# Fetching the selected value rows of the last 128 tokens instead of computing them densely

## What is computed

```python
v1, i1 = lax.top_k(s1, 16)          # per token and head, 8 heads
v2, i2 = lax.top_k(s2, 16)
...
eidx = take_along_axis(i1 * 128 + i2, pos)      # 16 experts of 16384 per head
g = jax.nn.softmax(top_s, axis=-1)
...
u = eu[it]                                      # 128 rows of 1024 per token
a = gelu(einsum('ckd,cd->ck', u, ht)) * gt
out = einsum('ck,ckd->cd', a, ev[it])           # 128 rows of 1024 per token
```

## Time and profile before

| | |
|---|---|
| median of 3 runs | 1881.18 us (1879.13 to 1882.46) |
| the profiled execution | 1878.64 us, its span 1876.9 us |
| mean granted clock of TensorE | 0.989 of full speed |
| instructions | 25250 |
| moved by DMA | 324.25 MB, mean 173 GB/s |

### The profile page before, as it was taken

One profiled execution on the slowest core, in us unless ns is written; L12 is line 12 of the kernel. 1 busy time (PEld: TensorE's weight loads), 2 busy tenths in 40 slices (PEclk: granted clock), 3 DMA queues, 4 the chain that ended last, 5 costly groups with the idle time before them and its releaser, 6 DMA issues.

```text
span 1876.9 us, 25250 instructions
## 1 busy us (share of the span) xinstructions
PE 1846.2 (98%) x8376; PEld 1511.2 (81%) x8376; DVE 1180.1 (63%) x1792; ACT 712.7 (38%) x938; POOL 762.4 (41%) x327
## 2 busy tenths in 40 slices
PE   5999998999999999999999999999999999999999
PEld 3876677888888888888888888888888888888887
DVE  7575557889990598989898983334434444334444
ACT  3544333334433444444454543232222322322321
POOL 4432223335444343333334344444444444444442
PEclk8999998999999999999999999999999999999999
DMA  7324343224444446464655467455665555665553
GB/s 272 135 80 142 133 151 135 91 79 144 148 145 150 135 163 224 168 218 162 223 179 207 173 212 256 164 196 185 201 204 182 195 190 184 198 203 191 195 180 116
DMA packets 159724, 324.25 MB, mean 173 GB/s; under 512 B 10816, under 2 KB 76480, under 8 KB 157504
## 3 DMA queue, kind: packets, MB, share of 16 engines
q1 hardware_dynamic: 159680, 323.70, 50.9%
HBM read 254.46 MB, written 69.21 MB: 172 GB/s over the span
## 4 chain that ended last, share of the span: by engine, by line
PE 95%; DVE 3%; DMA 1%; issue 0%; ACT 0%; DVEq 0%; SPq 0%; ACTq 0%; PEldq 0%
PE ps L1201 16%; PE ps L1202 16%; PE ps L1203 16%; PE ps L1478 12%; PE ps L1479 12%; PE ps L1477 12%; PE ps L1441 3%; DVE adasum L823 1%; PE ps L1330 1%; PE ps L1348 1%; PE ps L1412 1%; DMA ada<-w_ada 1%; PE ps L1270 1%; PE ps L1339 0%; DMA xt<-x_t 0%
## 5 line engine op out<-in xcount | busy, mean ns | idle before, releaser
L509 POOL TENSOR_TENSOR wlo<-raw,whi 128x1024 fp32r<-128x1024 f32 x304 | 750.5, 2470 | 1089.7 <-ACT whi L540 1089.7
L1201 PE MATMUL ps<-ahi,whi 128*128 128x512 f32 x1296 | 510.0, 394 | 0.2 <-DVE zbuf L917 0.2
L1202 PE MATMUL ps<-alo,whi 128*128 128x512 f32 x1296 | 507.6, 392 | 0.0
L1203 PE MATMUL ps<-ahi,wlo 128*128 128x512 f32 x1296 | 506.9, 391 | 0.0
L540 ACT ACTIVATE whi<-raw 128x1024 fp32r<-128x1024 f32 x304 | 323.6, 1065 | 464.3 <-PE ps L1479 432.1
L1152 DVE TENSOR_TENSOR prod<-gin,gates 128x512 f32<-128x512 f32 x128 | 179.0, 1399 | 403.3 <-DMA gin<-gelu_spill 400.2
L1478 PE MATMUL ps<-plo,whi 128*128 128x512 f32 x1024 | 398.8, 389 | 0.0
L1479 PE MATMUL ps<-phi,wlo 128*128 128x512 f32 x1024 | 398.8, 389 | 0.0
L1477 PE MATMUL ps<-phi,whi 128*128 128x512 f32 x1024 | 398.8, 389 | 0.0
L1203 PEld LDWEIGHTS ps<-ahi,wlo 128*128 128x128 f32 x1296 | 244.6, 189 | 51.6
L1201 PEld LDWEIGHTS ps<-ahi,whi 128*128 128x128 f32 x1296 | 244.9, 189 | 49.3 <-issue 0.7
(11 more groups left out here) (201 smaller groups left out, 1348.1 us busy)
## 6 DMA issues: line engine op xcount, KB each, us to landing
raw<-w_stream SPq DMA_DIRECT2D x304, 512.0 KB, 3.6
gelu_spill<-gout SPq DMA_DIRECT2D x128, 256.0 KB, 3.3
gate_spill<-gblock SPq DMA_DIRECT2D x16, 2048.0 KB, 7.3
gates<-gate_spill SPq DMA_DIRECT2D x32, 1024.0 KB, 7.0
gin<-gelu_spill SPq DMA_DIRECT2D x128, 256.0 KB, 3.8
ada<-w_ada SPq DMA_DIRECT2D x48, 512.0 KB, 5.3
xt<-x_t SPq DMA_DIRECT2D x1, 2048.0 KB, 7.9
out_t<-xt SPq DMA_DIRECT2D x8, 256.0 KB, 2.0
```

The costliest lines, as they stand in the source:

```text
L509: g.tensor_tensor(wlo[:, s, :], raw[:, s, :], whi[:, s, :].bitcast(F32), ALU.subtract)\
L1201: mm(out, shi, mhi, start=n == 0, stop=False)
L1202: mm(out, shi, mlo, start=False, stop=False)
L1203: last = mm(out, slo, mhi, start=False, stop=n == len(pairs) - 1)
```

## The change

The tokens are divided. Tokens 0 to 383 (`DENSE`) keep the dense last stage, with matmuls, products and loads over 384 columns in place of 512, and the scatter has 48 groups in place of 64, among 72 U chunks (`U_B` = 44, `U_C` = 116; 8 groups per 12). The U stage itself still covers all 512 tokens.

For tokens 384 to 511, which sit one to a partition, DVE works out two offsets for each of their 128 selected experts: the row of `w_front` that holds the expert_v row, and the place of its gelu value in `gelu_spill`. In the V stage POOL, after each subtraction, issues two indirect DMAs: `fetch_row(n)` brings expert n's row for each of the 128 tokens (128 x 4 KB) into one of `ROWS` = 8 buffers, `fetch_coef(n)` brings the 128 gelu values (4 bytes each). Row fetches begin at key 0, behind waits for the offsets, the scatter and the gate stores; coefficient fetches begin at key 4, once all gelu values are stored, two per key until they have caught up. DVE, five keys behind (`BEHIND`), multiplies gelu value and gate, and adds the scaled row to `acc`; in the last five keys it adds two. When all 128 are added (`row_added`), PE transposes `acc` into columns 384 to 511 of each bank, behind its last matmuls.

The gate spill is laid out by groups of four keys, so that a load reads 6 KB per partition in one piece, and a store writes pieces of 512 B.

```diff
--- before.py
+++ after.py
@@ -64,9 +64,15 @@
-U_A2, U_B, U_C = 36, 40, 120
-BODY_CHUNKS = 20
-BODY_GROUPS = 16
+DENSE = 3 * P
+FETCHED = TT - 1
+ROWS = 8
+BEHIND = 5
+U_A2, U_B, U_C = 36, 44, 116
+BODY_CHUNKS = 12
+BODY_GROUPS = 8
+GROUPS = DENSE // TOK_GROUP
 TAKE_GROUPS = 8
@@ -77,7 +83,7 @@
     gelu_dram = nc.dram_tensor("gelu_spill", (NK, P, T), F32).ap()
-    gate_dram = nc.dram_tensor("gate_spill", (T // TOK_BLOCK, P, NK * TOK_BLOCK), F32).ap()
+    gate_dram = nc.dram_tensor("gate_spill", (NK // GROUP, P, DENSE // TOK_BLOCK, GROUP * TOK_BLOCK), F32).ap()
@@ -197,11 +203,21 @@
-        gates = at("gates", 78, [P, 2, T // TOK_BLOCK, GROUP * TOK_BLOCK], F32)
-        gin = at("gin", 94, [P, RING, T], F32)
-        prod = at("prod", 8, [P, 2, T], F32)
-        phi = at("phi", 22, [P, RING, T], F32R)
-        plo = at("plo", 30, [P, RING, T], F32R)
+        gates = at("gates", 78, [P, 2, DENSE // TOK_BLOCK, GROUP * TOK_BLOCK], F32)
+        gin = at("gin", 94, [P, RING, DENSE], F32)
+        prod = at("prod", 8, [P, 2, DENSE], F32)
+        phi = at("phi", 22, [P, RING, DENSE], F32R)
+        plo = at("plo", 30, [P, RING, DENSE], F32R)
+        rows = at("rows", 38, [P, ROWS, D], F32)
+        acc = at("acc", 70, [P, D], F32)
+        expert = at("expert", 102, [P, 3, P], F32)
+        row_at = at("row_at", 103.5, [P, P], U32)
+        coef_at = at("coef_at", 104, [P, P], U32)
+        coef = at("coef", 104.5, [P, P], F32)
+        gate_of = at("gate_of", 105, [P, P], F32)
+        scaled = at("scaled", 105.5, [P, ROWS], F32)
+        token = sb("token", [P, 1], F32)
...
@@ -342,12 +363,12 @@
             t0 = s % GROUP * TOK_GROUP + half * 4
-            return gblock[:, s // GROUP % 2, :].rearrange("p (i t) -> p t i", t=TOK_BLOCK)[:, t0:t0 + 4, :]
+            return gblock[:, s // GROUP % 2, :].rearrange("p (i t) -> p i t", t=TOK_BLOCK)[:, :, t0:t0 + 4]
             both = ps[:, 2 * half:2 * half + 2, :].rearrange("p b (t n) -> p (b t) n", n=2 * NK)
-            return both[:, :, part * NK:(part + 1) * NK]
+            return both[:, :, part * NK:(part + 1) * NK].rearrange("p t n -> p n t")
@@ -418,7 +439,9 @@
                 sp.wait_ge(scat_added, 8 * b + 10)
-                sp.dma_start(gate_dram[b], gblock[:, buf, :]).then_inc(gate_stored[buf], 16)
+                sp.dma_start(gate_dram.rearrange("g p b n -> b p g n")[b],
+                             gblock[:, buf, :].rearrange("p (g n) -> p g n", n=GROUP * TOK_BLOCK))\
+                  .then_inc(gate_stored[buf], 16)
@@ -431,16 +454,14 @@
             def gin_load(e, s):
-                sp.dma_start(gin[:, s, :], gelu_dram[e]).then_inc(gin_in[s], 16)
+                sp.dma_start(gin[:, s, :], gelu_dram[e][:, 0:DENSE]).then_inc(gin_in[s], 16)
             def gate_load(g, buf):
-                sp.dma_start(gates[:, buf, :, :],
-                             gate_dram.rearrange("b p n -> p b n")[:, :, bass.ts(g, GROUP * TOK_BLOCK)])\
-                  .then_inc(gate_in[buf], 16)
+                sp.dma_start(gates[:, buf, :, :], gate_dram[g]).then_inc(gate_in[buf], 16)
             for b in range(2):
-                sp.wait_ge(gate_stored[b], 16 * (T // TOK_BLOCK // 2 + 1))
+                sp.wait_ge(gate_stored[b], 16 * (DENSE // TOK_BLOCK // 2 + 1))
             for b in range(2):
@@ -515,6 +536,10 @@
                             pattern=[[-1, HEADS], [0, P]], channel_multiplier=1).then_inc(consts, 1)
+            pool.wait_ge(consts, 15)
+            g.iota(token[:, :], [[0, 1]], base=FETCHED * P, channel_multiplier=1,
+                   allow_small_or_imprecise_dtypes=True).then_inc(token_ready, 1)
+            pool.wait_ge(token_ready, 1)
@@ -523,9 +548,39 @@
                          .then_inc(alo_first_ready, 1)
-            with pool.Fori(1, (C_E + NK) // RING) as i:
+            with pool.Fori(1, C_E // RING) as i:
                 for s in range(RING):
                     lo_part(i * RING + s, s)
+            def fetch_row(n):
+                if n >= ROWS:
+                    pool.wait_ge(row_added, n - ROWS + 1)
+                g.indirect_dma_start(rows[:, n % ROWS, :], None, w_front.rearrange("c p n -> (c p) n"),
+                                     bass.IndirectOffsetOnAxis(row_at[:, n:n + 1], 0)).then_inc(row_in[n % ROWS], 16)
+            def fetch_coef(n):
+                g.indirect_dma_start(coef[:, n:n + 1], None,
+                                     gelu_dram.rearrange("e p (t o) -> (e p t) o", o=1),
+                                     bass.IndirectOffsetOnAxis(coef_at[:, n:n + 1], 0)).then_inc(coef_in[n % ROWS], 16)
+            for e in range(NK):
+                lo_part(C_E + e, e % RING)
+                if e == 0:
+                    pool.wait_ge(places_ready, 1)
+                    pool.wait_ge(scat_done, 4 + 2 * GROUPS)
+                    for b in range(2):
+                        pool.wait_ge(gate_stored[b], 16 * (DENSE // TOK_BLOCK // 2 + 1))
+                fetch_row(e)
+                if e == RING:
+                    for s in range(RING):
+                        pool.wait_ge(gelu_stored[s], 16 * (NK // RING + 1))
+                if RING <= e < ROWS:
+                    for n in (2 * (e - RING), 2 * (e - RING) + 1):
+                        fetch_coef(n)
+                elif e >= ROWS:
+                    fetch_coef(e)
@@ -721,7 +776,7 @@
                     act.wait_ge(slots_done, 1)
-                    a.activation(gate_hi[:, :], ps[:, 2, :], ACT.Copy).then_inc(gate_hi_ready, 1)
+                    a.activation(gate_hi[:, 0:DENSE], ps[:, 2, 0:DENSE], ACT.Copy).then_inc(gate_hi_ready, 1)
@@ -1086,11 +1141,21 @@
                             ALU.mult).then_inc(gates_ready, 1)
+            fetched = [picked[:, k, FETCHED * P:T] for k in range(3)]
+            dve.wait_ge(token_ready, 1)
+            v.scalar_tensor_tensor(expert[:, 0, :], fetched[0], float(NK), fetched[1], ALU.mult, ALU.add)
+            dve.drain()
+            v.tensor_scalar(expert[:, 1, :], expert[:, 0, :], float(C_E * P), None, ALU.add)
+            v.tensor_scalar(expert[:, 2, :], expert[:, 0, :], float(T), token[:, 0:1], ALU.mult, ALU.add)
+            v.tensor_copy(gate_of[:, :], fetched[2])
+            dve.drain()
+            v.tensor_copy(row_at[:, :], expert[:, 1, :])
+            v.tensor_copy(coef_at[:, :], expert[:, 2, :]).then_inc(places_ready, 1)
             dve.wait_ge(slots_done, 1)
             for k in range(2):
-                v.tensor_copy(slots[:, k, :], ps[:, k, :]).then_inc(slots_taken, 1)
+                v.tensor_copy(slots[:, k, 0:DENSE], ps[:, k, 0:DENSE]).then_inc(slots_taken, 1)
             dve.wait_ge(gate_hi_ready, 1)
-            v.tensor_tensor(gate_lo[:, :], ps[:, 2, :], gate_hi[:, :].bitcast(F32), ALU.subtract)\
+            v.tensor_tensor(gate_lo[:, 0:DENSE], ps[:, 2, 0:DENSE], gate_hi[:, 0:DENSE].bitcast(F32), ALU.subtract)\
              .then_inc(slots_taken, 1)
@@ -1137,7 +1202,7 @@
             make_onehots(0, 0)
-            takes = T // TOK_GROUP // TAKE_GROUPS
+            takes = GROUPS // TAKE_GROUPS
             with dve.Fori(0, takes - 1) as i:
@@ -1162,22 +1227,49 @@
-            dve.wait_ge(scat_done, 4 + 2 * (T // TOK_GROUP))
+            def add_row(n, q, s):
+                dve.wait_ge(row_in[s], 16 * (q + 1))
+                dve.wait_ge(coef_in[s], 16 * (q + 1))
+                column = slice(n, n + 1) if isinstance(n, int) else bass.ds(n, 1)
+                v.tensor_tensor(scaled[:, s:s + 1], coef[:, column], gate_of[:, column], ALU.mult)
+                dve.drain()
+                if isinstance(n, int) and n == 0:
+                    v.tensor_scalar(acc[:, :], rows[:, s, :], scaled[:, s:s + 1], None, ALU.mult).then_inc(row_added, 1)
+                else:
+                    v.scalar_tensor_tensor(acc[:, :], rows[:, s, :], scaled[:, s:s + 1], acc[:, :],
+                                           ALU.mult, ALU.add).then_inc(row_added, 1)
+            def last_rows(s):
+                done = NK - 8 - BEHIND + s + max(0, s - (8 - BEHIND))
+                return range(done, done + (1 if s < 8 - BEHIND else 2))
+            dve.wait_ge(scat_done, 4 + 2 * GROUPS)
             for e in range(2):
                 make_prod(None, 0, e)
-            with dve.Fori(0, NK // 8 - 1) as i:
+            for e in range(8):
+                prod_lo(e, e)
+                gates_landed((e + 2) // 8, (e + 2) % 8)
+                make_prod(e + 2, (e + 2) // RING, (e + 2) % 8)
+                if e >= BEHIND:
+                    add_row(e - BEHIND, 0, e - BEHIND)
+            with dve.Fori(1, NK // 8 - 1) as i:
                 for s in range(8):
                     make_prod(i * 8 + n, i * 2 + n // RING, n % 8)
+                    add_row(i * 8 + (s - BEHIND), i + (s - BEHIND) // 8, (s - BEHIND) % 8)
             for s in range(8):
                     make_prod(e + 2, (e + 2) // RING, (e + 2) % 8)
+                for n in last_rows(s):
```

(20 more changed lines are left out.)

## The result

The changed kernel takes 1895.5 us (median of 4 runs, 1890.89 to 1896.27) against 1880.16 for the kernel before beside it: a ratio of 1.0077, 95% interval 1.0064 to 1.0089. It is slower by 15 us where 65 fewer were forecast. The profiled execution took 1896.27, its span 1894.5. One execution of all those in this document (the fourth of the tenth experiment: 2788.6 us, mean granted clock 0.65, where the others have 0.99) was in a slower state and is left out.

The account below looks back on a forecast made before the run. PE bounds the kernel before; afterwards POOL's and DVE's shared access, 5.1 us per key. Scatter -15, last stage -56, start and end +6: -65 from 1878.6 gives 1814, or 1816 us at the median; range 1778 to 1915.

Parts of the forecast that it names:

- B: POOL's queue, last stage: the fetches' issue cost decides; past 1.35 us each POOL sets the pace; chance 0.26.
- D: Last stage: a fetch also excludes DVE's two-input work; 7.4 us per key, 2110 us; chance 0.05.
- PE's part: Last-stage matmuls over 384 columns: 0.173 us each, 4.15 us per key in place of 5.44.
- The scatter: Scatter on PE's path: 48 groups in place of 64, 15 us less.
- The gate store with 512 B pieces: Gate spill store: lands in 7 to 14 us, costing zero, or a few us per store if its cover fails.
- +6 us for start and end: Last stage's first coefficient fetches and its final row adds and transposes: 6 us added together, 0 to 15.
- The fetches: POOL's queue, last stage: two indirect DMAs per key, taken at 1.2 us each.
- POOL's sum: POOL's own work per key in the last stage: 2.39 subtraction plus 2.4 fetches, 4.8 us.
- The shared access: Last stage: POOL's subtraction (2.39) and DVE's two-input work (2.6) exclude each other; with handover 5.1 us per key.
- three sums of work: Last stage: a key takes the largest of PE 4.15, POOL 4.8 and shared access 5.1 us.
- rival C: Last stage: gin's landing grows from 3.8 to about 8.8 us; loop of 16 us, 5.35 per key, 1848; chance 0.05.

Follow-up runs that it names:

- the tenth experiment: Changed kernel with subtraction on DVE, gin and gates requested two keys earlier ahead of the weight load, and the old gate spill layout: 1702.8 us.
- the sixth experiment: Changed kernel with POOL's subtraction moved to DVE, and gin and gates requested two keys earlier, ahead of the weight load: 1701.8 us, ratio 0.9052.
- eighth: Changed kernel with gin and gates requested two keys earlier, ahead of the weight load, and without the coefficient fetches: 1777.9 us, ratio 0.9452.
- seventh: Changed kernel with gin and gates requested two keys earlier, ahead of the weight load, POOL still subtracting: 1818.8 us, ratio 0.9673.

## Why the prediction was wrong

**The time.** 1816 was forecast, 1778 to 1915 given, 1895.5 measured: inside the range, on the other side. None of the rivals that end slower came true: fetches did not cost too much (B), and did not exclude DVE for their length (D).

**PE's part was right.** 384 columns take 0.173 us, a key 4.15; in the sixth experiment, where nothing else binds, a key takes 4.17. The scatter gave its 15 us. The gate store with 512 B pieces landed in 7.6 us and stopped nothing. Of the +6 us for start and end, the end took none: from the last L1570 to the end of the span are 4.3 us, 4.1 before the change.

**The fetches were right in size.** 1.2 each was taken, 1.05 and 1.22 measured on average. A fetch takes 0.94 us, or longer if an operation of DVE on two SBUF tiles is running as it begins: then by what is left of that operation, less 0.12. With 0.27 left it takes 1.10, with 0.96 left 1.77, and so it is for nearly all of 1168 fetches in the last stages of five runs:

```profile
1409.01 1.28 DVE L1240 SCALAR_TENSOR_TENSOR acc<-rows,scaled,acc 128x1024 f32<-128x1024 f32 x1
...
1409.33 1.77 POOL L563 DMA_INDIRECT coef<-gelu_spill,coef_at  x1 [0.30 <-issue]
```

An operation that begins after the fetch does not lengthen it: in the sixth, 112 row fetches take 0.94 each with DVE's subtraction begun 0.05 us behind them. Left out of POOL's sum were the gaps, 0.16 and 0.30 ahead of the two: POOL needs 5.09, not 4.8.

**The bound was the wrong one, at nearly the right number.** The shared access was taken to set 5.1 us per key. It sets 4.75 (eighth); POOL's queue sets 5.09 (seventh). That the two terms erred in opposite ways is why the forecast of 1816 is within 3 us of the seventh experiment, and proves nothing for the step that led to it. The exclusion itself, read from the earlier trace rows, is shown. The Trainium skill, "SBUF — State Buffer" (Who interferes with whom), states it for a DVE instruction with two SBUF inputs beside a GpSimd instruction that reads SBUF; the 3.36 and 2.75 us above agree. Taken at its word for the whole length of a fetch it gave case D, 7.4 us per key. Measured, a fetch only waits for the rest of the DVE operation that runs when it begins, 0.8 us beside the row add of 1409.01, and that row add takes its 1.28 all the same.

**The step that failed** is the key's time as the largest of three sums of work (PE 4.15, POOL 4.8, shared access 5.1), with every loop of waits held to be shorter: rival C, where it was priced. It says that the loop "subtraction, gin, product, phi, whi, subtraction three keys on needs 8.8 + 0.3 + 0.55 + 0.5 + 1.06 + 2.4 + 2.4 = 16 us", at a landing of 8.8 us, and is "still faster", with a chance of 0.05. Landings did not grow (gin's median is 3.4, 3.7 before), and a key takes 5.67. The loop that binds has other members. It takes the product at its bare 0.55, while the exclusion just argued for makes it 2.7. It leaves DVE by phi and not by the row add behind the product, so the new work (the add's 1.3, the row fetch that waits for a buffer, 1.6 with its gaps, and the coefficient fetch, 1.8) is not in it. And it starts from the median landing, where the kernel issues a gates load ahead of every fourth gin: 6.35. With these the turn is 17.5 us for three keys. Its own way, by phi and whi, is there too, in 9 of the 27 turns; but between plo and whi stands a whole key of PE, which it leaves out, and the turn takes 23.1 us for four keys. Each operation was priced as work; DVE's and POOL's were compared as sums per key; but neither engine can work ahead when the order of its queue ties it to the other's last result. The earlier trace rows had shown it: DVE waited for gin before 97 of 128 products, and that wait was hidden because PE needed 5.44 us for a key.

## To carry to other kernels

Where an engine takes on new work in a pipelined loop, sum not only each engine's work per step but each ring of waits, divided by the number of steps that it spans; include what stands behind a wait in the same queue, and the request that stands behind another's wait. A wait that is hidden today is the first candidate: give its request more lead before the work is added, and move work between engines only after that. The order of three requests decided here between 0.8% slower and 3% faster, and with the subtraction moved between 22% slower and 9.5% faster.

## What was not expected of the hardware

The order of elements in the scatter's copies matters. With tokens innermost, so that `gblock` is written in runs of four, ACT's copy of 512 values takes 598 ns and DVE's add 682, about half. The groups of the page before, then the two lines after:

```profile
L1125 DVE TENSOR_TENSOR gblock<-gblock,ps 128x512 f32<-128x512 f32 x128 | 151.4, 1233 | 54.4 <-ACT gblock L731 54.4
...
L731 ACT ACTIVATE gblock<-ps 128x512 f32<-128x512 f32 x128 | 132.8, 1154 | 0.0
```

```profile
L786 ACT ACTIVATE gblock<-ps x96: 592/598/608, 672.8 to 1100.1; 128x512 f32<-128x512 f32 x96
```

```profile
L1190 DVE TENSOR_TENSOR gblock<-gblock,ps x96: 677/682/689, 673.4 to 1100.9; 128x512 f32<-128x512 f32 x96
```

No run changes this order alone; the two engines, of which DVE adds to `gblock` and ACT only writes it, both show it.

An indirect DMA of 128 rows of 4 KB occupies POOL as long as one of 128 values of 4 bytes: 0.94 to 0.96 us either way when no two-input operation of DVE runs as it begins.

The last stage of the sixth experiment moved 336 GB/s at a DMA share of 0.93 without slowing PE, with loads, gathers and pieces of several sizes mixed.
